# Values of heads 4 to 7 by block products for two heads at once, with the last modulation chunks moved behind the last softmax

## The reference

```python
mod = silu(c) @ ada_w + ada_b                       # 2048 x 12288 weights, 100 MB
sh1, sc1, g1, sh2, sc2, g2 = split(mod, 6)
h = rms_norm(x, norm1_g) * (1 + sc1) + sh1
q, k, v = split(h @ da_w_in, 3)                     # 2048 x 6144; 8 heads of 256 columns each in q, k, v
for each head: p_i = softmax(q_i k_i^T - slope * dist), i = 0, 1
               o = (p_0 - lam * p_1) @ v            # 256 x 256
o = rms_norm(o) * (1 - lam_init)
x = x + g1 * (o @ da_w_out)                         # 2048 x 2048
hf = rms_norm(x, norm2_g) * (1 + sc2) + sh2
x = x + g2 * moe(hf)                                # 32 experts of 2048 x 1024 and 512 x 2048: 403 MB
out = rms_norm(x, final_g)
```

## Time and profile before

| | |
|---|---|
| median of 3 runs | 1484.15 us (1481.45 to 3825.19) |
| profiled execution, its own time | 1485.01 us |
| its span | 1483.3 us |
| PE busy | 1160.1 us, 78% |
| DVE busy | 632.2 us, 43% |
| moved by DMA | 577.92 MB, 390 GB/s over the span |
| chain that ended last | PE 58%, DMA 33%, DVE 5% |

### The profile page before, as it was taken

The page is one execution under the profiler, slowest core; times in us unless marked ns, Lnnn a source line. Parts: engine busy times, 40 slices in busy tenths (PEclk is TensorE's granted clock), DMA queues, the critical chain, the costliest instruction groups (busy, mean ns, idle before and its releaser), DMA issues.

```text
span 1483.3 us, 20520 instructions
## 1 busy us (share of the span) xinstructions
PE 1160.1 (78%) x8500; PEld 744.6 (50%) x8500; DVE 632.2 (43%) x1001; ACT 179.1 (12%) x401; POOL 66.6 (4%) x82
## 2 busy tenths in 40 slices
PE   5999999999999998867577567668558568657765
PEld 5888878888888885334133124224214224224322
DVE  5766688877747424552132132124114114213214
ACT  3011152221134110300000000000000000000002
POOL 0000111111100000000000000000000000000001
PEclk9999999999999999979789789779879878887868
DMA  9999999999997477999999999999999999999996
GB/s 335 386 386 355 400 333 385 389 395 387 344 369 276 164 294 327 427 404 398 429 426 429 429 427 430 427 429 429 426 429 428 429 429 427 429 428 428 427 427 264
DMA packets 128523, 577.92 MB, mean 390 GB/s; under 512 B 10346, under 2 KB 59584, under 8 KB 102868
## 3 DMA queue, kind: packets, MB, share of 16 engines
q1 hardware_dynamic: 110592, 507.84, 85.0%
q0 software_dynamic: 17680, 69.21, 12.0%
q10 hardware_dynamic: 196, 0.09, 0.0%
HBM read 575.02 MB, written 2.10 MB: 389 GB/s over the span
## 4 chain that ended last, share of the span: by engine, by line
PE 58%; DMA 33%; DVE 5%; ACT 1%; issue 1%; ACTq 0%; SPq 0%; DVEq 0%
DMA ring<-in_moe_w_gu_dram 26%; PE psum L782 11%; PE psum L1156 9%; PE psum L746 7%; DMA ring<-in_moe_w_d_dram 7%; PE psum L1063 5%; PE psum L1185 4%; PE psum L756 4%; PE psum L1208 4%; PE psum L974 3%; PE psum L895 2%; PE psum L887 2%; PE psum L718 1%; PE psum L693 1%; DVE arena L1983 1%
## 5 line engine op out<-in xcount | busy, mean ns | idle before, releaser
L1156 PE MATMUL psum<-ring,ada_ring 128*32 128x256 f32 x3696 | 274.5, 448 | 144.3 <-DMA ring<-in_moe_w_gu_dram 144.3
L1156 PEld LDWEIGHTS psum<-ring,ada_ring 128*32 128x32 f32 x3696 | 125.6, 121 | 288.9 <-DMA ring<-in_moe_w_gu_dram 189.6
L1185 PE MATMUL psum<-ring,arena 128*32 128x512 f32 x960 | 157.3, 803 | 27.7 <-ACT arena L1458 15.5
L1982 DVE TENSOR_SCALAR arena<-arena 128x128 f32<-128x128 f32 x32 | 7.3, 227 | 354.2 <-ACT arena L1452 354.1
L1999 DVE TENSOR_TENSOR arena<-psum,arena 32x512 f32<-32x512 f32 x108 | 74.1, 686 | 186.3 <-PE psum L1185 177.6
L782 PE MATMUL psum<-region_b,ring 128*128 128x256 f32 x512 | 118.8, 391 | 4.3 <-ACT region_b L1318 4.3
L746 PE MATMUL psum<-region_b,ring 128*128 128x256 f32 x512 | 112.0, 379 | 0.0
L782 PEld LDWEIGHTS psum<-region_b,ring 128*128 128x128 f32 x512 | 100.1, 197 | 19.4 <-issue 4.5
L1452 ACT ACTIVATE arena<-psum 128x128 f32<-128x128 f32 x32 | 8.9, 277 | 781.4 <-PE psum L1156 736.0
L746 PEld LDWEIGHTS psum<-region_b,ring 128*128 128x128 f32 x512 | 96.7, 190 | 12.8
L1185 PEld LDWEIGHTS psum<-ring,arena 128*32 128x32 f32 x960 | 37.3, 135 | 124.6 <-issue 83.7
(11 more groups left out here) (272 smaller groups left out, 1087.2 us busy)
## 6 DMA issues: line engine op xcount, KB each, us to landing
ring<-in_moe_w_gu_dram SPq DMA_DIRECT2D x123, 2048.0 KB, 25.6
ring<-in_moe_w_d_dram SPq DMA_DIRECT2D x62, 2048.0 KB, 24.2
ada_ring<-in_ada_w_dram POOLq DMA_DIRECT2D x64, 1024.0 KB, 10.1
ada_ring<-in_ada_w_dram SPq DMA_DIRECT2D x24, 1024.0 KB, 11.0
ring<-in_da_w_in_dram SPq DMA_DIRECT2D x12, 2048.0 KB, 47.1
ring<-in_da_w_in_dram SPq DMA_DIRECT2D x21, 1024.0 KB, 14.2
ring<-in_da_w_out_dram SPq DMA_DIRECT2D x8, 2048.0 KB, 19.9
ada_ring<-in_ada_w_dram SPq DMA_DIRECT2D x16, 512.0 KB, 9.0
```

The lines of the kernel that those rows point to most:

```text
L1156: last = mm(psum[32 * n:32 * n + 32, B_GU, 0:256].rearrange("p (a b) -> p a b", a=2), x_items[:, k, SLOTS * i:SLOTS * (i + 1)], w[:, :, n ...
L1185: last = mm(psum[32 * n:32 * n + 32, B_D + i % 2, :], hid_t[:, k, :], w[:, kk, n, :], start=k == 0, stop=k == FT - 1)
```

## The change

1. The values of two heads, 4 and 5, then 6 and 7, are made together from two ring slots that hold the rows 0 to 1023 and 1024 to 2047 of 512 columns (`v_pair`). Seven block products of 8 matmuls take the place of eight such for each pair. DVE makes four sums of h once, four differences of weight blocks for each pair, and joins the products; ACT copies three partial results for each pair to a new buffer `pieces`. The loads are reordered (`W_ORDER`).
2. Chunks of the modulation come later on DVE: 83 are done at the end of `combine` of head 7, and the last five behind s1 to s4. `sum_rows`, `turn_rows` and `keep_mod` move with them. The load of x again stays behind the last chunk's load on POOL's queue. The gate is spread, and group 7 turned, inside the first `two_chunks`.
3. The descriptor memory of POOL's DMAs is 8 KB for each partition where the default had 16 KB. `pieces` takes these 8 KB.
4. A fifth 2 MB quarter has a whole spare place (`pieces` and one slot of `ada_ring`), so the ring is one slot ahead from expert 2 on.
5. The router's weights come with 2 DMAs in place of 8, and DVE multiplies them as two tiles.

The core of the diff:

```diff
-SPARE = ((0, 3), (1, 0), (1, 1), (1, 2))
+SPARE = ((0, 3), (1, 0), (1, 1), (1, 2), (1, 3))
+SCRATCH = 8192
+        pieces = sb("pieces", [P, CH // 2])
-        GATE1_BANK = (B_V, B_S, B_S + 1, B_MOD)
+        GATE1_BANK = (B_S, B_V, B_S + 1, B_V)
+        W_ORDER = ((4, 0), (4, 1), (4, 2), (5, 2), (5, 0), (5, 1), (6, 0), (6, 1), (6, 2), (7, 2), (7, 0), (7, 1))
...
             gp.wait_ge(mod_summed, FIRST_WIDE + WIDE - 1)
+            gp.wait_ge(w_used, w_at(7, 2) + 1)
             gp.dma_start(x_nat, x[0].rearrange("(a p) d -> p a d", p=P)).then_inc(x_again, 16)
...
+            def v_pair(h, sums):                                     # PE
+                p = (h - 4) // 2
+                b11, b12, b21, b22 = v_blocks(p)
+                n = w_at(h, 2)
+                pe.wait_ge(w_loaded[n % RING], w_turn(n))
...
+                v_product(U_BANK, 0, h11, b11).then_inc(v_done, 1)
+                pe.wait_ge(w_loaded[(n + 1) % RING], w_turn(n + 1))
+                pe.wait_ge(qkv_ready, qk_copied(h, 0))
+                pe.wait_ge(h_sums, 4)
+                v_product(XY, Y_AT, hs4, b22).then_inc(v_done, 1)
+                attend(h - 1, 1)
+                v_product(XY, X_AT, h12, b21).then_inc(v_done, 1)
+                pe.wait_ge(v_sums, 4 * p + 3)
+                pe.wait_ge(v_kept, 3 * p + 1)
+                v_product(U_BANK, 0, hs2, b22, start=False).then_inc(v_done, 1)
+                scores(h, 0)
+                pe.wait_ge(v_kept, 3 * p + 2)
+                v_product(U_BANK, 0, hs3, b12, start=False).then_inc(v_done, 1)
+                v_product(Z_BANK, 0, hs1, b11).then_inc(v_done, 1)
+                sums()
+                pe.wait_ge(v_sums, 4 * p + 4)
+                pe.wait_ge(v_kept, 3 * p + 3)
+                v_product(U_BANK, 0, h22, b21, start=False).then_inc(w_used, 2)
...
-            out_part(0, 0, done_k - 2)
+            out_part(0, 0, 6)
+            transpose_out(last_head - 1)
+            out_part(0, 6, done_k - 2)
+            turn_rows(WIDE - 3)
             transpose_probs(last_head)
             out_part(0, done_k - 2, done_k)
             attend(last_head, 1)
             out_loaded(1)
             out_part(1, 0, 6)
             transpose_out(last_head)
             out_part(1, 6, 10)
-            sum_rows(WIDE - 1)
+            sum_rows(WIDE - 2)
             out_part(1, 10, done_k)
+            turn_rows(WIDE - 2)
...
-            pe.wait_ge(diag_ready, 1)
-            pe.wait_ge(qkv_ready, QKV_CH - 6)
-            turn_rows(WIDE - 1)
-            for i, b in enumerate(GATE1_BANK):
-                if b == B_MOD:
-                    pe.wait_ge(mod_ready, 24)
-                spread_diag(i, b)
+            def spread_gate1():
+                pe.wait_ge(diag_ready, 1)
...
+                for i, b in enumerate(GATE1_BANK):
+                    if i == 3:
+                        pe.wait_ge(gate_ready, 2)
+                    spread_diag(i, b)
                 block_product(bank["s4b22"], s4, c2, 8).then_inc(block_done, 1)
                 if p == 0:
-                    pe.wait_ge(gate_ready, 4)
-                    pe.wait_ge(bias_parted, 1)
-                    mm(psum[:, B_MOD, 0:36], ones[:], bias_part, start=True, stop=True).then_inc(bias_spread, 1)
+                    sum_rows(WIDE - 1)
+                    spread_gate1()
+                    turn_rows(WIDE - 1)
...
                 keep_block(kept_p1, bank["u"])                       # ACT
+                if p == 0:
+                    keep_rows(WIDE - 1)
+                    for n, b in enumerate(GATE1_BANK):
+                        keep_gate1(n, b)
...
-            head(7, 84, between=5, ahead=1)                          # DVE
-            keep_mod(6)
-            add_bias(HEADS - 1)
-            combine(HEADS - 1)
-            chunks(93, 2)
-            out_rstd(HEADS - 1)
-            chunks(95, 1)
+            v_pair(6)
+            chunks(72, 6)
+            keep_mod(4)
+            chunks(78, 5)
+            out_rstd(6)
+            add_bias(7)
+            combine(7)
+            chunks(83, 3)
+            keep_mod(5)
+            chunks(86, 2)
+            out_rstd(7)
+            chunks(88, 3)
             step.link(v.tensor_tensor(s3, a11, a21, ALU.subtract))
             v.tensor_tensor(s4, a12, s2, ALU.subtract).then_inc(blocks_ready, 1)
             dve.wait_ge(blocks_ready, 1)
+            chunks(91, 2)
+            keep_mod(6)
+            chunks(93, 3)
...
+            by_router(router_wa, a2[:]).then_inc(router_scaled, 1)
+            dve.wait_ge(mod_summed, FIRST_WIDE + WIDE)
+            step.link(by_router(bias_parts, mod[:, SH2:SH2 + KT]))
             v.reduce_sum(bias_part, bias_parts.rearrange("p k n -> p n k"), X).then_inc(bias_parted, 1)
             dve.wait_ge(bias_parted, 1)
+            keep_mod(WIDE - 1)
...
-    nc = _bacc.Bacc("TRN2", target_bir_lowering=False, num_devices=1)
+    nc = _bacc.Bacc("TRN2", target_bir_lowering=False, num_devices=1, dynamic_dma_scratch_size=SCRATCH)
```

More of the change, by code:

```diff
@@ L149, in encoder_layer @@
         kept_p1, kept_u2, kept_p5, kept_p4 = carve(4096, VD), carve(4352, VD), carve(5120, VD), carve(6144, VD)
+        h11, h12 = h_t[:, 0:8, 0:P], h_t[:, 8:16, 0:P]
+        h21, h22 = h_t[:, 0:8, P:T], h_t[:, 8:16, P:T]
+        hs1, hs2, hs4 = (held[:, 1024 * i:1024 * (i + 1)].rearrange("p (k t) -> p k t", k=8) for i in range(3))
+        hs3 = pieces[:, 0:1024].rearrange("p (k t) -> p k t", k=8)
+        v_p1, v_u2, v_u3 = (pieces[:, 1024 + VD * i:1024 + VD * (i + 1)] for i in range(3))
         o_items = carve(0, D)
@@ L489, in load_item @@
                     s = moe_slot(m, turn)
[L490 to L493 removed]
+                    if j < 4:
                         sp.dma_start(ring[:, s, :].rearrange("p (j x) -> p j x", j=1),
@@ L763, in head @@
             def head(h, par, sums, between=None):
-                qk_product(h, par, 0, between)
+                qk_product(h, 0, between)
                 sums[0]()
                 transpose_probs(h - 1)
-                qk_product(h, par, 1)
+                qk_product(h, 1)
                 sums[1]()
-                attend(h - 1, 1 - par)
-                v_product(h, par)
-                sums[2]()
-                scores(h, par)
-                transpose_out(h - 1)
+                if par == 0:
+                    v_pair(h, sums[2])
+                    transpose_out(h - 1)
+                else:
+                    attend(h - 1, 0)
+                    sums[2]()
+                    scores(h, 1)
@@ L1137, in moe_group @@
                         spare = SPARE.index((i, j)) if first and (i, j) in SPARE else None
-                        halved = first and (i, j) == HALF_SPARE
                         if i == 0 and j < 3:
@@ L1295, in copy_out, with v_pair, head @@
                       scale=vcols[:, SUB_G + half:SUB_G + half + 1]).then_inc(ot_copied, 1)
-            def head(h, par, sums, out_late=False):
-                exps(h - 1)
+            def v_pair(h, sums=None):
+                p = (h - 4) // 2
+                act.wait_ge(v_done, 6 * p + 1)
+                A(v_p1, psum[:, U_BANK, 0:VD], ACT.Copy).then_inc(v_kept, 1)
+                norm_out(h - 1)
+                act.wait_ge(v_done, 6 * p + 4)
+                A(v_u2, psum[:, U_BANK, 0:VD], ACT.Copy).then_inc(v_kept, 1)
+                act.wait_ge(v_done, 6 * p + 5)
+                A(v_u3, psum[:, U_BANK, 0:VD], ACT.Copy).then_inc(v_kept, 1)
+                exps(h)
+                if sums is not None:
+                    keep_rows(sums)
+                act.wait_ge(w_used, w_at(h + 1, 2) + 1)
+                A(v_tok[:, 0, 1, :], psum[:, U_BANK, 0:VD], ACT.Copy).then_inc(v_copied, 1)
+            def head(h, par, sums, out_late):
                 if out_late:
@@ L1666, in keep_rest, with sum_h @@
                                        in1=part_sum(h - 2, j), op0=ALU.mult, op1=ALU.add).then_inc(rest_ready, 1)
-            def head(h, first, between=None, behind=None, ahead=4):
-                add_bias(h - 1)
-                combine(h - 1)
-                chunks(first, 4)
-                if between is not None:
-                    keep_mod(between)
-                chunks(first + 4, 4)
-                if behind is not None:
-                    keep_mod(behind)
-                out_rstd(h - 1)
-                chunks(first + 8, ahead)
+            def sum_h():
+                dve.wait_ge(parts_added, 6)
+                v.tensor_tensor(hs1, h21, h22, ALU.add).then_inc(h_sums, 1)
+                dve.wait_ge(h_sums, 1)
+                v.tensor_tensor(hs2, hs1, h11, ALU.subtract).then_inc(h_sums, 1)
+                dve.wait_ge(h_sums, 2)
+                v.tensor_tensor(hs4, h12, hs2, ALU.subtract).then_inc(h_sums, 1)
+                v.tensor_tensor(hs3, h11, h21, ALU.subtract).then_inc(h_sums, 1)
@@ L1707, in _ @@
             keep_mod(0)
-            head(4, 48, behind=1)
-            head(5, 60, between=2)
-            keep_mod(3)
```

(26 more changed lines are left out.)

198 lines of the change are left out of this document (122 added, 76 removed).

## The result

The changed kernel takes 1499.37 us (median of 4 runs, 1497.02 to 1499.93). The kernel before takes 1482.8 us (median of 4 runs, of which one took 3825.19 us and does not count in the ratio). The ratio is 1.0107, 95% interval 1.0092 to 1.0122: some 16 us slower. The forecast was 1497 us in a range of 1481 to 1504. The profiled execution took 1499.82 us, its span is 1498.1: 14.8 us over that of before.

The account below looks back on a forecast made before the run. PE was taken to bound the kernel up to the second expert group, DMA after. U2 moving from 471.9 to 485.5 gave +13.6 us, taken as +13: 1498 profiled, 1497 as median, range 1481 to 1504.

Parts of the forecast that it names:

- What bounds it: Up to the second expert group PE bounds, then DMA; a shift at U2 goes through to the end.
- Heads: Attention heads: two value pairs save 6.9 us of PE; head 7's scores end at 416.2, `combine` at 423.0.
- The tight place: Inside a value pair, PE's wait for DVE's third subtraction: DVE through at 11.5 us, PE asks at 12.1, holds by 0.6.
- The late chain: Behind the heads: chunks, x's load, ACT's copies, gate, turn of group 7, subtractions; U2 at 485.5, +13.6 us.
- part of the waits may not come: Late chain: some waits for chunk loads may not come, so +13 us was taken where the sum gave +13.6.
- The shorter chains beside it: Beside x's chain: chunk 95 to spreads at 471, some 5 us ahead of ACT; PE stalls of 3 and 6 us.
- Who sets U2: First `two_chunks`: DVE's three subtractions are queued behind `keep_mod`'s wait for the turn of group 7; U2 at 485.5.
- The ring, the router, the fifth spare quarter: Half the descriptor memory, 2 router loads instead of 8, and 2 MB brought forward: each put at nothing.
- The clock: PE at 1.2 GHz behind new pauses at 458 and 472 us, under DVE's subtractions: 0, at most 2 us.
- Hidden: Chunks, x and gate ready when PE asks: U2 at 463.7 to 466.7, -5 to -8 us; chance 0.08.
- Half hidden: x lands before about 459 or ACT is not last; chunk 95 sets U2 at 474 to 480, -2 to +8; chance 0.12.
- Worse: Value pairs stall too, or x takes 16.1 us: above +20 us, 1505 and more; chance 0.07.

Follow-up runs that it names:

- e12: Changed kernel with one modulation chunk of each value pair (54 and 72) placed between `add_bias(h)` and `combine(h)`: ratio to the kernel before 1.0112.
- e1: Changed kernel with x's load on ACT's queue behind `keep_rows(6)`, not on POOL's behind chunk 95: ratio to the kernel before 1.0120.
- e11: e9 with a modulation chunk in each value pair and s1 to s4 between chunks 88 and 89: ratio to the kernel before 1.0025.
- e2: Changed kernel with DVE's three subtractions ahead of its wait in `keep_mod(7)` for the turn of group 7: ratio to the kernel before 1.0084.
- e4: Kernel before with the 8 KB descriptor ring of the change and nothing else: ratio to the kernel before 1.0007.
- e7: Changed kernel with x on ACT's queue, subtractions ahead of the `keep_mod(7)` wait, and `a12b21` ahead of the sum of group 7: ratio to the kernel before 1.0085.
- e5: Kernel before with one added wait that keeps x's second load on POOL's queue behind s1 to s4: ratio to the kernel before 1.0047.
- e9: Changed kernel, x on ACT's queue, `out_rstd(7)` one chunk earlier, diagonals early, U2 before gate spreads, subtractions between chunks 92 and 93: ratio to the kernel before 1.0059.

## Why the prediction was right

*What bounds it.* Right. The loss at U2 (+15.5 us) came through to the end (+14.8), and the dip of DMA ahead of the second group of experts moved from 665 to 680 us.

*Heads.* Right. The scores of head 7 ended at 415.1 (416.2 forecast), `combine` at 421.8 (423.0). In both value pairs PE runs through without a pause; in the first, DVE's second and fourth subtractions wait 0.9 and 0.6 us for PE, not the other way. The tight place held by 0.3 us (third subtraction done at 273.7, PE there at 273.99) where the sum had 0.6.

*The late chain.* Right in every link. Chunk 90 ended at 448.1 (446.5 forecast), x was issued at 457.1 (455.5), the copies ran from 466.9 (466.1), the turn was done at 480.0 (478.4), U2 began at 487.4 (485.5). That these differ by only 0.8 to 1.9 us is in part luck, since larger errors cancel. `combine` of head 7 was 1.2 us early. The wait for chunk loads is the term that was mis-sized: 2.1 us were added, and chunks 87, 89 and 90 waited 3.04, 1.36 and 0.76, 5.2 in sum. x itself landed in 9.8 us (10.6), near the lower bound as argued. The clock, below, added 1.1. What I had not seen about the loads is that DVE frees no buffer during the softmax of head 7, so that POOL waits 8.5 us before it can issue chunk 87. The empty stretches in the value pairs are not the cause: chunks 83 to 86 found their data there, and filling part of the stretches (e12) moved nothing. Nor did "part of the waits may not come" hold, the reason for taking +13 and not +13.6: U2 moved by 15.5.

*The shorter chains beside it.* The pause at `transpose_out(7)` was 3.9 us (3), the one for chunk 95 6.4 (6). But the chain chunk 95, diagonal, spreads was put at 5 us ahead of ACT, and was 3.1 us ahead: chunk 95 ended 1.6 us later, and six spread instructions took 4.26 us at half the clock. e1 shows what this margin means. With x gone early, only 1.6 us of the turn come free. The prediction named x as the chain that sets U2, and it is; but it did not say that chunk 95 alone would cost nearly as much. So x is neither the whole loss nor a fixed share of it, and most of the loss came back only when x was early and the queues of DVE and PE were in another order too (e11).

*Who sets U2.* Right that the subtractions stand behind the wait of `keep_mod(7)`; e2 takes it away, and some 3 us come off, 2.2 of them by the order. In the prediction that looked like a link of one chain; it was a free choice of order.

*The ring, the router, the fifth spare quarter.* At nothing, and right as far as tested: e4 shows it for the ring. In the changed kernel GpSimd's issues have a mean of 728 ns, where they had 720. The router's loads and the quarter were not tried alone.

*The clock.* Put at 0, at most 2 us, since the slow pieces lie under DVE's subtractions. For `a12b21` that held: it took 5.34 instead of 3.70 us, and PE still waited 2.0 us for U2. For the fourth spread and the turn it did not, since these stand ahead of the subtractions: they took 2.3 us (477.54 to 479.84, clock 0.50) where the same two took 1.2 at full clock in e2. So the clock cost 1.1 us of the chain, within the bound. In e1 and e7, where U2 followed a pause of 3.5 to 3.7 us, it cost 1.7 us of U2 and `s1t1`. In e5 it is a third of the 7.4 us: `a12b21` took 6.29.

*The rivals.* Hidden: no; DVE did not end chunk 95 before 466.4, as was held against it (464; without any wait for loads the same sum gives 462, so "whatever DMA does" said too much). Half hidden, x landed before 459: not in this kernel, but e1 is that case, and its price was wrong there: U2 at 485.5 instead of 474 to 480. Its "-2 to +8" is a slip: 474 is 2 us behind 471.9, not ahead, so the range's lower end of 1481 stood some 4 us too low. (The low bound of the main sum, 480.1, is 480.7 by the terms that it names.) Neither decided anything. Worse: the pairs did not stall.

## What to carry to other kernels

Saved matmuls are worth what the next engine leaves of them: here 6.9 us of TensorE were bought with 27 us on VectorE, and making one product twice again cost only about 4. When work is moved behind a point, follow every queue entry behind it, loads too: a load of x that depends on none of the moved work cost 7.4 us in the kernel before as soon as it went out late. And when two chains end within a few microseconds, removing one shows nothing; make the experiment from the other side as well (delay it alone in the kernel before), then reorder both.

## What the runs showed of the hardware

*A small VectorE operation blocked by GpSimd.* `by_router` on 128x64 elements took 3.53 us at 466.68, with GpSimd's diagonal (3.60 us) started at 466.53. With the diagonal made early (e9) the same operation took 0.23 us, and the 3.6 us were paid elsewhere: in e11 the diagonal runs at 387.35, and five halves of chunks beside it took 10.02 us where five take 6.5. So moving it beside busy VectorE work saves nothing on VectorE's sum, it only takes it off the late chain. Beside an idle VectorE it is free: in e5 the diagonal ran at 451.87, within a pause of 4.89 us in which VectorE waited for PE.

The Trainium skill ("SBUF — State Buffer", SBUF: two separate sides) says that VectorE, when it reads two operands from SBUF, and a GpSimd operation that reads SBUF lock one port pair for the whole instruction, and the other one blocks fully. The trace agrees: 3.53 us is the length of the neighbour, not of the work.

*A load that competes.* x's 2 MB landed in 8.0 us with no chunk load beside it (e5), in 9.8 when issued behind the last chunk load, and in 12.7 when issued 12 us earlier beside them (e1), and the chunks behind it then waited 2.3 us more.

*The clock behind pauses.* The same 32 matmuls (U2 and `s1t1`) took 7.15 us in the changed kernel and 8.83 in e1; the same 16 of `a12b21` 3.62 (e1), 5.34 (changed kernel) or 6.29 (e5). Behind the changed kernel's pause of 6.40 us the granted clock in 465 to 470 us was 0.50 of full speed, 1.2 GHz.
